# Joins before the feed-forward stages: post-norm, norm and scaling as separate steps in another order

## The chip, the cores and the metric

The kernel runs on one core of a Trainium2 chip. The metric is the device time of one execution in microseconds (us). A core has five engines that this text names: PE (TensorE, the matrix engine), DVE (VectorE), ACT (ScalarE), POOL (GpSimd) and SP (SyncE, which here only issues DMAs). Each works through its own list of instructions in order, and semaphores tie the lists together.

## The reference

Two transformer blocks run one after the other on 256 tokens of width 1024, all in float32. Only the ends of the mixers and the feed-forward parts matter here:

```
def rms_norm(x, g):
    xf = x.astype(jnp.float32)
    y = xf * lax.rsqrt(jnp.mean(xf * xf, axis=-1, keepdims=True) + NORM_EPS)
    return (y * g.astype(jnp.float32)).astype(x.dtype)

# first block (272 tokens until the mixers, 256 after)
mixed = (gate_a * y_a + gate_b * y_b) @ w_out[l]
h = h + rms_norm(mixed, mix_post_g[l])
u = rms_norm(h, ffn_pre_g[l])
gt, up = jnp.split(u @ w_ffn_in[l], 2, axis=-1)
h = h + rms_norm((jax.nn.silu(gt) * up) @ w_ffn_out[l], ffn_post_g[l])

# second block
x = x + _rms_norm(mix @ w_out[l], attn_post_norm[l])
h = _rms_norm(x, ffn_pre_norm[l])
x = x + _rms_norm(_conv_ffn(h, ffn_w_gate[l], ffn_w_up[l], ffn_conv_w[l], ffn_conv_b[l], ffn_w_down[l]), ffn_post_norm[l])
```

`_conv_ffn` is `(gelu(conv3(h @ w_gate) + b) * (h @ w_up)) @ w_down` with 4096 hidden columns.

## The kernel before

**Weights.** Every float32 product is made from parts: a weight `w` is split into `hi` (a copy rounded to fp32r) and `lo = w - hi`, and likewise each activation. Weights come from memory in slabs of 128x2048 into three buffers `raw0` to `raw2`; each half of a slab is a **unit** (128x1024, eight 128x128 blocks). For each unit u one engine makes `hi` (tile `wh`, "copy") and another makes `lo` (tile `wl`, "subtraction"). The string `MADE` says who: `d` is lo on DVE and hi on ACT, `p` lo on POOL and hi on ACT, `v` both on DVE, `q` lo on POOL and hi on DVE. The step `("split", u)` is where both are issued. SP asks for slab s+3 when both units of slab s are split.

**Order.** One list, `ORDER`, of named steps is walked by every engine's function (`tensor`, `scalar`, `vector`, `gpsimd`, `sync`); each emits its own part of a step. So the place of a step in the list fixes its place on every engine. The list is woven by `weave` from a main line (matmul steps) and side chains, by the strings in `MIX`, where a dot takes the next main step and a letter the next step of a chain.

**The joins.** Each of the four output products (`out1`, `ffn1`, `out2`, `ffn2`) ends in a join. Tokens come in two halves c = 0, 1 of 128 and columns in two halves h = 0, 1 of 512. For each c the chain made by `chains` is:

- `post(c,0)`, `post(c,1)`: ACT squares the accumulator (tile `pb`) and sums the row; DVE makes a partial mean (128x1) and multiplies the accumulator by the output factors (`FA<-pb,post`); after h = 1 ACT takes the square root and DVE the reciprocal.
- `res(c)`: DVE adds the scaled product to the residual, `X<-FA,st,X`, two instructions.
- `norm(c)`: ACT squares both halves of X, DVE makes the partial mean, ACT the root, DVE the reciprocal; then ACT scales the first half (`FA<-X,st`) and DVE the second.
- `turn(x,c)`: PE transposes the scaled rows (8 matmuls, line L509); `op(x,c,0)`, `op(x,c,1)`: ACT makes eight 128x128 `hi` parts (`R<-pb,sm`), DVE eight `lo` parts (`R<-pb,sm,R`).

PE meanwhile ends the output product with four `tail(name,c,h)` steps of 12 matmuls, then does `turn(x,0)`, then `gemm0` of the first four feed-forward tiles with token half 0 only (32 matmuls of 256 columns), then `turn(x,1)`, then `gemm1` of the same four tiles (64 matmuls). After that come full tiles of 16 matmuls, `gemm(g2,i)` and `gemm(u2,i)`, and from i = 4 on a `down` of 12.

**The tiles' banks.** Gate and up tiles of the second feed-forward go round four PSUM banks. Tile i+2 takes the bank that tile i had, and waits until step `hidden(i)` has emptied it: ACT copies one half of the bank, DVE adds the other (`FA<-pb,FA`), first for the gate tile and, three instructions later, for the up tile. `hidden(0)` comes in the list after the splits that stand behind the join.

## Time and profile before

| | |
|---|---|
| median of 3 runs | 923.08 us (923.01 to 923.38) |
| the profiled execution | 922.91 us |
| its span, first to last instruction | 921.1 us |
| PE busy | 901.0 us, 98% of the span |
| DVE, ACT, POOL busy | 671.3 us (73%), 466.2 us (51%), 214.1 us (23%) |
| mean granted clock of PE | 0.997 of full speed |
| join `out1` into the first feed-forward | about 316 to 334 us |
| join `out2` into the second feed-forward | about 631 to 650 us |

The page of the profile lists each engine's busy time; a timeline lists instructions in order of time, equal neighbours merged; windows give busy time and granted clock of a stretch. "Idle before" in brackets is how long the engine stood still ahead of a row and who let it go.

### The profile page before, as it was taken

The page shows a single profiled execution, that of the slowest core. Times are in us where ns is not written, and L with a number is a line of the kernel's source. Part 1 is how long each engine was busy: PE and PEld are TensorE (multiplying, and loading weights), DVE is VectorE, ACT ScalarE, POOL GpSimd, SP SyncE. Part 2 cuts the span into 40 slices and gives each one's busy share as a digit, 9 for nine tenths or more (in the row PEclk, how much of TensorE's full clock was granted, in tenths as well). Part 3 has the DMA queues.
Part 4 walks back from the last instruction along what each step waited for, and adds up shares of the span by engine and source line. Part 5 has one row for each costly group of instructions (what it writes and reads, how often), then busy time and mean ns, then how long its engine had stood idle before and what let it go on. Part 6 is the DMA issues. An engine that isn't in the chain of part 4 may idle for free.

```text
span 921.1 us, 16817 instructions
## 1 busy us (share of the span) xinstructions
PE 901.0 (98%) x6767; PEld 799.8 (87%) x6767; DVE 671.3 (73%) x1277; ACT 466.2 (51%) x937; POOL 214.1 (23%) x116
## 2 busy tenths in 40 slices
PE   8999999999999999999999999999999999999996
PEld 8879999989999888888888799877988888888885
DVE  6625987557656888766676668858888888788885
ACT  7443336555443574444435647776634445544343
POOL 4123421531222210652214342231101211210121
PEclk9999999999999999999999999999999999999999
DMA  8535443333333645656545354224445555455531
GB/s 318 197 138 184 139 164 114 115 116 136 117 138 132 231 163 190 221 183 223 190 162 203 137 204 164 96 79 180 166 168 195 183 197 210 153 217 183 214 106 46
DMA packets 23181, 153.67 MB, mean 167 GB/s; under 512 B 2864, under 2 KB 3248, under 8 KB 5568
## 3 DMA queue, kind: packets, MB, share of 16 engines
q1 hardware_dynamic: 22384, 150.43, 45.9%
q0 software_dynamic: 576, 2.10, 0.6%
q8 instruction: 54, 0.88, 0.4%
q14 instruction: 23, 0.19, 0.1%
q10 hardware_dynamic: 144, 0.07, 0.0%
HBM read 151.28 MB, written 1.05 MB: 165 GB/s over the span
## 4 chain that ended last, share of the span: by engine, by line
PE 62%; DVE 24%; ACT 9%; issue 4%; DMA 0%; DVEq 0%; SPq 0%; ACTq 0%
PE pb L506 60%; DVE wl L515 10%; ACT wh L512 4%; DVE FA L515 4%; DVE FA L521 4%; ACT FA L512 3%; DVE FA L518 3%; PE pb L509 2%; DVE wh L530 1%; ACT R L512 1%; DVE X L521 1%; DVE R L521 1%; DVE st L518 0%; DMA X<-in_x 0%; DVE FA L524 0%
## 5 line engine op out<-in xcount | busy, mean ns | idle before, releaser
L506 PE MATMUL pb<-R,wh 128*128 128x256 f32 (+2 forms) x2224 | 550.4, 326 | 4.5 <-ACT R L512 2.0
L506 PE MATMUL pb<-R,wl 128*128 128x256 f32 (+1 forms) x1512 | 422.6, 281 | 0.0
L506 PEld LDWEIGHTS pb<-R,wh 128*128 128x128 f32 x2224 | 372.3, 189 | 43.8 <-ACT R L512 3.5
L515 POOL TENSOR_TENSOR wl<-raw,wh 128x1024 fp32r<-128x1024 f32 (+1 forms) x76 | 185.1, 2439 | 635.7 <-ACT wh L512 513.0
L515 DVE TENSOR_TENSOR wl<-raw,wh 128x1024 fp32r<-128x1024 f32 (+1 forms) x202 | 266.9, 1343 | 84.5 <-ACT wh L512 82.8
L506 PEld LDWEIGHTS pb<-R,wl 128*128 128x128 f32 x1512 | 284.3, 188 | 2.1 <-issue 0.4
L512 ACT ACTIVATE wh<-raw 128x1024 fp32r<-128x1024 f32 (+1 forms) x220 | 223.8, 1044 | 52.4 <-PE pb L506 50.1
L506 PE MATMUL pb<-wh,R 128*128 128x512 f32 (+2 forms) x724 | 234.4, 388 | 3.4 <-DVE R L515 2.1
L506 PEld LDWEIGHTS pb<-wh,R 128*128 128x128 f32 (+1 forms) x724 | 134.4, 186 | 35.9 <-ACT R L512 4.0
L512 ACT ACTIVATE FA<-pb 128x256 f32<-128x256 f32 (+7 forms) x240 | 94.0, 414 | 124.3 <-PE pb L506 113.2
L506 PE MATMUL pb<-wl,R 128*128 128x512 f32 (+2 forms) x372 | 143.4, 385 | 0.0
L512 ACT ACTIVATE FA<-FA 128x256 f32<-128x256 f32 (+4 forms) x69 | 28.0, 405 | 139.7 <-DVE FA L521 121.8
L515 DVE TENSOR_TENSOR FA<-pb,FA 128x256 f32<-128x256 f32 (+1 forms) x128 | 53.9, 427 | 34.7 <-ACT FA L512 34.7
L506 PEld LDWEIGHTS pb<-wl,R 128*128 128x128 f32 (+1 forms) x372 | 68.2, 183 | 12.5
L515 DVE TENSOR_TENSOR FA<-FA 128x256 f32<-128x256 f32 (+7 forms) x120 | 68.7, 597 | 8.2 <-ACT FA L512 2.6
L506 PE MATMUL pb<-FA 128*32 128x16 f32 (+6 forms) x1456 | 60.9, 216 | 0.2
L512 ACT ACTIVATE R<-FA 128x256 fp32r<-128x256 f32 (+1 forms) x66 | 28.4, 431 | 61.7 <-DVE FA L515 61.7
L506 PEld LDWEIGHTS pb<-FA 128*32 128x32 f32 (+3 forms) x1456 | 53.0, 132 | 7.0 <-issue 1.7
L530 DVE CAST wh<-raw 128x1024 fp32r<-128x1024 f32 (+1 forms) x58 | 44.4, 768 | 13.1 <-PE pb L506 13.1
L515 DVE TENSOR_TENSOR R<-FA,R 128x256 fp32r<-128x256 f32 (+1 forms) x58 | 26.9, 464 | 28.9 <-ACT R L512 28.9
L512 ACT ACTIVATE FA<-FA,st 128x256 f32<-128x256 f32 (+2 forms) x65 | 29.3, 453 | 9.8 <-DVE st L518 9.6
L521 DVE SCALAR_TENSOR_TENSOR FA<-FA,sm 128x255 f32<-128x255 f32 x64 | 31.0, 484 | 2.3
(122 smaller groups left out, 462.0 us busy)
## 6 DMA issues: line engine op xcount, KB each, us to landing
raw<-in_w SPq DMA_DIRECT2D x137, 1024.0 KB, 4.8
X<-in_x SPq DMA_DIRECT2D x2, 512.0 KB, 4.3
raw<-in_w SPq DMA_DIRECT2D x2, 512.0 KB, 6.6
post<-in_ffn_post SPq DMA_DIRECT2D x2, 512.0 KB, 4.5
post<-in_w POOLq DMA_DIRECT2D x2, 512.0 KB, 5.1
FA<-in_w POOLq DMA_DIRECT2D x2, 512.0 KB, 8.2
out<-X SPq DMA_DIRECT2D x4, 256.0 KB, 2.0
cst<-in_cst SPq DMA_DIRECT2D x1, 821.5 KB, 12.3
```

The costliest lines, as they stand in the source:

```text
L506: return self.real.matmul(*a, **k) if self.real else self
L509: return self.real.transpose(*a, **k) if self.real else self
L512: return self.real.activation(*a, **k) if self.real else self
L515: return self.real.tensor_tensor(*a, **k) if self.real else self
L518: return self.real.tensor_scalar(*a, **k) if self.real else self
L521: return self.real.scalar_tensor_tensor(*a, **k) if self.real else self
L530: return self.real.tensor_copy(*a, **k) if self.real else self
```

## The change

The step `post` is cut in two. What stays in `post` is ACT's square with its sum (and the root after h = 1) and DVE's partial mean; the multiplication by the output factors and the reciprocal become `gain`. The step `norm` is cut in two: the squares, partial mean and root stay, and the reciprocal and both scalings become `scaled`. The new strings of `MIX` place these steps; in `ffn1` and `ffn2` the parts follow one another as before, in `out1` and `out2` they don't. A table `LATE` moves the subtraction of two units (87 and 183) behind another step. In `MADE`, unit 183 goes from `v` to `d`: its copy is now ACT's.

```
-    return [[("post", name, c, 0), ("post", name, c, 1), ("res", name, c)]
-            + ([("norm", name, c), ("turn", x, c), ("op", x, c, 0), ("op", x, c, 1)] if x else []) for c in range(2)]
+    return [[("post", name, c, 0), ("gain", name, c, 0), ("post", name, c, 1), ("gain", name, c, 1), ("res", name, c)]
+            + ([("norm", name, c), ("scaled", name, c), ("turn", x, c), ("op", x, c, 0), ("op", x, c, 1)] if x else [])
+            for c in range(2)]
...
-    "out1": "............c.cac..aacbab.a.aa..bb.bcbbcc.c...",
+    "out1": "............c.caac..aaacabab.abb.aa.b.bb.bcbbcc.c...",
...
-    "out2": "c.cac.a.a.aca.bcaa..bbc.bbcbbc....",
-    "ffn2": "aaa..b.bb.",
+    "out2": "c.caac.aa.ac.aababbb.aa.b.bb.bcbbcc.c...",
+    "ffn2": "aaaaa..bb.bbb.",
...
+LATE = {87: ('norm', 'out1', 0), 183: ('scaled', 'out2', 0)}
+for _u, _s in LATE.items():
+    ORDER.insert(ORDER.index(_s) + 1, ("low", _u))
...
+                elif kind == "scaled":
+                    name, c = a
+                    x = {"out1": "x2", "ffn1": "x3", "out2": "x4"}[name]
                     e.wait_ge(*dve.at(("rstd", x, c)))
                     e.activation(fa(2048 + 1024 * c, 512), X[:, 1024 * c:1024 * c + 512], ACT.Identity,
                                  scale=stat(("rstd", x, c))).then_inc(*act.up(("xn", x, c, 0)))
...
+            def low(a):
+                u = a[0]
+                c, _, hi = unit_cols(a)
+                e.wait_ge(*(act if hi == "act" else dve).at(("hi", *a)))
+                e.tensor_tensor(WL[PLACE[u]][:, c], rawu(u)[:, c], rf(WH[PLACE[u]][:, c]),
+                                ALU.subtract).then_inc(*dve.up(("lo", *a)))
...
-                    if lo == "dve":
-                        e.wait_ge(*(act if hi == "act" else dve).at(("hi", *a)))
-                        e.tensor_tensor(WL[PLACE[u]][:, c], rawu(u)[:, c], rf(WH[PLACE[u]][:, c]),
-                                        ALU.subtract).then_inc(*dve.up(("lo", *a)))
+                    if lo == "dve" and u not in LATE:
+                        low(a)
+                elif kind == "low":
+                    low(a)
...
                 elif kind == "post":
                     name, c, h = a
+                    if h == 0:
+                        e.wait_ge(*act.at(step))
+                        e.tensor_scalar(stat(("post_part", name, c)), stat(("post_ss", name, c), 2)[:, 0:1], 1.0 / D, EPS,
+                                        ALU.mult, ALU.add).then_inc(*dve.up(("post_part", name, c)))
+                elif kind == "gain":
+                    name, c, h = a
                     e.wait_ge(*in_post[name].at("all"))
                     e.wait_ge(*pe.at(("tail", name, c, h)))
-                    e.wait_ge(*act.at(step))
-                    if h == 0:
-                        e.tensor_scalar(stat(("post_part", name, c)), stat(("post_ss", name, c), 2)[:, 0:1], 1.0 / D, EPS,
-                                        ALU.mult, ALU.add).then_inc(*dve.up(("post_part", name, c)))
+                    e.wait_ge(*act.at(("post", name, c, h)))
                     e.tensor_tensor(fa(1024 * c + 512 * h, 512), acc(name, c, h)[:, :], post[:, 512 * h:512 * h + 512],
                                     ALU.mult).then_inc(*dve.up(("gained", name, c, h)))
                     banks.ended(("acc", name, c, h), dve.now())
```

PE's and POOL's own lists stay as they are, instruction for instruction. The splits of units 184 to 188 stand elsewhere. In the list before: 184 ahead of `op(x4,0)`, 185 ahead of `norm(out2,1)`, 186 between `turn(x4,1)` and `op(x4,1)`, then 187 and 188 behind. In the list after: 184 between `turn(x4,1)` and `op(x4,1)`, then 185, 186, 188, 187 behind. Units 184 and 186 have their subtraction on POOL, 185, 187 and 188 on DVE; 186 has its copy on DVE, the others on ACT.

**DVE in `out1`**, from the residual of token half 0 to the scaling of that half (pb6 and pb7 are the accumulators of half 1, wl7 is unit 87). Before:

```order
L521 SCALAR_TENSOR_TENSOR X<-FA,st,X 128x512 x2
L515 TENSOR_TENSOR wl7<-raw1,wh7 128x1024
L518 TENSOR_SCALAR st<-st 128x1
L515 TENSOR_TENSOR FA<-pb6,post 128x512
L518 TENSOR_SCALAR st<-st 128x1
L533 RECIPROCAL st<-st 128x1
L518 TENSOR_SCALAR FA<-X,st 128x512
L515 TENSOR_TENSOR FA<-pb7,post 128x512
```

And after, at the same place:

```order
L525 SCALAR_TENSOR_TENSOR X<-FA,st,X 128x512 x2
L522 TENSOR_SCALAR st<-st 128x1
L519 TENSOR_TENSOR wl7<-raw1,wh7 128x1024
L522 TENSOR_SCALAR st<-st 128x1
L537 RECIPROCAL st<-st 128x1
L522 TENSOR_SCALAR FA<-X,st 128x512
L519 TENSOR_TENSOR FA<-pb6,post 128x512
L519 TENSOR_TENSOR FA<-pb7,post 128x512
```

The norm's partial mean now stands ahead of the subtraction, and the factors of pb6 behind the scaling.

**DVE in `out2`**, from the operands of token half 0 to the first instruction of `hidden(0)` (`FA<-pb,FA`). Before:

```order
L521 SCALAR_TENSOR_TENSOR R<-pb,sm,R 128x128 x8
L515 TENSOR_TENSOR FA<-pb,post 128x512
L533 RECIPROCAL st<-st 128x1
L521 SCALAR_TENSOR_TENSOR X<-FA,st,X 128x512 x2
L515 TENSOR_TENSOR wl<-raw,wh 128x1024
L518 TENSOR_SCALAR st<-st 128x1
L533 RECIPROCAL st<-st 128x1
L518 TENSOR_SCALAR FA<-X,st 128x512
L530 CAST wh<-raw 128x1024
L521 SCALAR_TENSOR_TENSOR R<-pb,sm,R 128x128 x8
L515 TENSOR_TENSOR wl<-raw,wh 128x1024 x2
L515 TENSOR_TENSOR FA<-pb,FA 128x256
```

And after:

```order
L525 SCALAR_TENSOR_TENSOR R<-pb,sm,R 128x128 x8
L525 SCALAR_TENSOR_TENSOR X<-FA,st,X 128x512 x2
L522 TENSOR_SCALAR st<-st 128x1
L537 RECIPROCAL st<-st 128x1
L522 TENSOR_SCALAR FA<-X,st 128x512
L525 SCALAR_TENSOR_TENSOR R<-pb,sm,R 128x128 x8
L519 TENSOR_TENSOR wl<-raw,wh 128x1024
L534 CAST wh<-raw 128x1024
L519 TENSOR_TENSOR wl<-raw,wh 128x1024 x2
L519 TENSOR_TENSOR FA<-pb,FA 128x256
```

The last factors and their reciprocal went ahead of the first operands; one subtraction (unit 185) and one copy (unit 186) went from ahead of the second operands to behind them.

## Rows read from the trace of the kernel before

**Rows 1.** The page's part 1, PE: busy us, share of span, instructions.

```profile
PE 901.0 (98%) x6767; PEld 799.8 (87%) x6767; DVE 671.3 (73%) x1277; ACT 466.2 (51%) x937; POOL 214.1 (23%) x116
```

**Rows 2.** Windows: stretch, us, busy by engine, granted clock, DMA share, GB/s.

```profile
643.70:646.60 2.90, 2.90 (x14) 2.90 (x15) 2.87 (x5) 2.46 (x6) 0.00 (x0) 0.50 0.44 184
...
908.00:910.00 2.00, 2.00 (x10) 1.68 (x9) 0.75 (x2) 0.21 (x2) 0.00 (x0) 1.00 0.00 0
```

**Rows 3.** Timeline of PE: start us, us, engine, line, operation; idle before in brackets.

```profile
327.35 4.99 PE L506 MATMUL pb<-R,wh 128*128 128x256 f32 x32 [0.69 <-DVE R L521]
...
639.41 1.04 PE L509 MATMUL pb<-cst,FA 128*128 128x128 f32 x8
641.90 6.37 PE L506 MATMUL pb<-R,wh 128*128 128x256 f32 x32 [1.45 <-ACT R L512]
648.42 1.09 PE L509 MATMUL pb<-cst,FA 128*128 128x128 f32 x8
```

**Rows 4.** Timeline of PE: starts of gate tile 2 and up tile 4; a late idle.

```profile
657.56 0.40 PE L506 MATMUL pb<-R,wh 128*128 128x512 f32 x1
...
671.70 0.40 PE L506 MATMUL pb<-R,wh 128*128 128x512 f32 x1
...
906.56 0.47 PE L506 MATMUL pb<-wh,R 128*128 128x512 f32 x1 [2.10 <-DVE R L515]
```

**Rows 5.** Timeline of ACT in join `out1`.

```profile
322.55 0.62 ACT L512 ACTIVATE FA<-X 128x512 f32<-128x512 f32 x1
...
324.79 0.72 ACT L512 ACTIVATE FA<-X,st 128x512 f32<-128x512 f32 x1 [0.23 <-DVE st L533]
```

**Rows 6.** Timeline of DVE in join `out1`.

```profile
320.89 1.42 DVE L521 SCALAR_TENSOR_TENSOR X<-FA,st,X 128x512 f32<-128x512 f32 x2
...
326.86 2.14 DVE L521 SCALAR_TENSOR_TENSOR R<-pb,sm,R 128x128 fp32r<-128x128 f32 x8
```

**Rows 7.** Timeline of ACT in join `out2`.

```profile
638.48 0.72 ACT L512 ACTIVATE FA<-X,st 128x512 f32<-128x512 f32 x1 [0.23 <-DVE st L533]
...
639.68 1.05 ACT L512 ACTIVATE wh<-raw 128x1024 fp32r<-128x1024 f32 x1
...
647.64 0.72 ACT L512 ACTIVATE FA<-X,st 128x512 f32<-128x512 f32 x1 [0.23 <-DVE st L533]
648.89 2.17 ACT L512 ACTIVATE R<-pb,sm 128x128 fp32r<-128x128 f32 x8 [0.53 <-PE pb L509]
```

**Rows 8.** Timeline of DVE in join `out2`.

```profile
635.75 1.41 DVE L521 SCALAR_TENSOR_TENSOR X<-FA,st,X 128x512 f32<-128x512 f32 x2
...
641.41 2.15 DVE L521 SCALAR_TENSOR_TENSOR R<-pb,sm,R 128x128 fp32r<-128x128 f32 x8
643.61 0.69 DVE L515 TENSOR_TENSOR FA<-pb,post 128x512 f32<-128x512 f32 x1
...
644.40 1.42 DVE L521 SCALAR_TENSOR_TENSOR X<-FA,st,X 128x512 f32<-128x512 f32 x2
645.73 1.22 DVE L515 TENSOR_TENSOR wl<-raw,wh 128x1024 fp32r<-128x1024 f32 x1
```

**Rows 9.** Timeline of DVE behind join `out2`: `hidden(0)` and, last row, `hidden(2)`.

```profile
652.04 2.44 DVE L515 TENSOR_TENSOR wl<-raw,wh 128x1024 fp32r<-128x1024 f32 x2 [0.59 <-ACT wh L512]
654.40 0.42 DVE L515 TENSOR_TENSOR FA<-pb,FA 128x256 f32<-128x256 f32 x1
...
669.77 0.42 DVE L515 TENSOR_TENSOR FA<-pb,FA 128x256 f32<-128x256 f32 x1
```

**Rows 10.** Timelines of DVE and POOL: a copy and two subtractions meet POOL.

```profile
883.37 0.69 DVE L530 CAST wh<-raw 128x1024 fp32r<-128x1024 f32 x1
884.09 4.56 DVE L515 TENSOR_TENSOR wl<-raw,wh 128x1024 fp32r<-128x1024 f32 x2
...
884.03 2.40 POOL L515 TENSOR_TENSOR wl<-raw,wh 128x1024 fp32r<-128x1024 f32 x1 [23.32 <-ACT wh L512]
...
648.81 2.38 POOL L515 TENSOR_TENSOR wl<-raw,wh 128x1024 fp32r<-128x1024 f32 x1 [5.65 <-DVE wh L530]
```

More of the change, by code:

```diff
@@ L412 @@
 MADE = ("dpdpddddddddqdpdpdddpddpvpvdppqpdddppddddpddvqpqpqpdpdvddpdddpqddvdpddppddpddpddpddvvdddqvddddpd"
-        "ddvvvdvdppdpdppvvpdqpdpqvddpvpdvpdddvpdvpdvdddvqdddqqpddpdpvddvdddddddpvvvdppvpppdvvdddvpdqddddd"
+        "ddvvvdvdppdpdppvvpdqpdpqvddpvpdvpdddvpdvpdvdddvqdddqqpddpdpvddvdddddddpvvvdppvpppdvvddddpdqddddd"
         "pvddvddddvdddvdpqpdddddddqddddddddddddddppddpddddddqddddvddvdvddddddpdvvdddvdvpdddpp")
@@ L418 @@
     "latent": "...a.......a..a...........a.b....b.fgf.b..e.f.g.e.dc.f.ba...c.ge.i.cg.ecdh.dh....i...i.h.d.ih",
-    "out1": "............c.cac..aacbab.a.aa..bb.bcbbcc.c...",
-    "ffn1": "..aaa..aa..c....caac....bbc..b..b..b.b...b............",
+    "out1": "............c.caac..aaacabab.abb.aa.b.bb.bcbbcc.c...",
+    "ffn1": "..aaaaa..aaa..c....caac....bbbbc..b..bb..b.b...b............",
     "maps": "...a.....acbabcbc..cc.bbb.ede.eed.ecag.agcdgcggadc.b.bfcgbefdc.ab.dgfbe.dbhffbab.hcfhcccf.ghiecb"
             "eif.gahf.ddib.b.bbigchjbj.i.cbcibhhcjkhajkhckkhcjbiiibjcbijkicjgikc.kjjjkk.kkijg.k.",
-    "out2": "c.cac.a.a.aca.bcaa..bbc.bbcbbc....",
-    "ffn2": "aaa..b.bb.",
+    "out2": "c.caac.aa.ac.aababbb.aa.b.bb.bcbbcc.c...",
+    "ffn2": "aaaaa..bb.bbb.",
 }
@@ L1888, in vector @@
                     x = {"out1": "x2", "ffn1": "x3", "out2": "x4"}[name]
-                    r = stat(("rstd", x, c))
                     e.wait_ge(*act.at(("norm", name, c, 0)))
@@ L1892, in vector @@
                                     ALU.mult, ALU.add).then_inc(*dve.up(("norm_part", x, c)))
+                elif kind == "scaled":
+                    name, c = a
+                    x = {"out1": "x2", "ffn1": "x3", "out2": "x4"}[name]
+                    r = stat(("rstd", x, c))
                     e.wait_ge(*act.at(("sd", x, c)))
```

## The prediction

> **What bounds the kernel now.** I read first the page's busy times: PE is busy 98% of the span [rows 1], so only what makes PE stand still, or stretches its work, can move the time. Next I listed who PE waited for, stretch by stretch. Inside the two feed-forward stages that list is empty but for the last tiles; PE stands in the joins. In `out1` it stands ahead of the first transposes and again 0.69 us before `gemm0`; the 32 matmuls of `gemm0` then take 4.99 us. In `out2` it stands 1.45 us, and the same 32 matmuls take 6.37 us [rows 3]. Windows laid over that stretch say why: from 643.70 to 646.60 the granted clock is 0.50, so PE ran at 1.2 GHz and not at 2.4 [rows 2]; it is the only such place while PE works. What PE had done before was to transpose (1.04 us) [rows 3], to stand 1.45 us, and to go at the pace of the operands for two more. The price is 6.37 - 4.99 = 1.4 us, but it was nearly hidden: the transposes of token half 1 start at 648.42 [rows 3], and the scaled rows were not there until 647.64 + 0.72 = 648.36 anyhow [rows 7].
>
> So each join has two halves: until `gemm0` starts, and until `turn(x,1)` starts. After that comes a third thing, how far DVE is behind PE at the start of the feed-forward, and there the change puts new work.
>
> **Part 1, join `out1`.** Before, ACT squared X from 322.55 and scaled it at 324.79 [rows 5]; DVE had begun X at 320.89 [rows 6], then came a subtraction (1.22 us, as in rows 8), the factors of pb6 and the partial mean. With nothing in between, the path from X to scaling takes 638.48 - 635.75 = 2.73 us [rows 7, 8], so scaling could come at 323.62: the gain is at most 1.17 us, and at least nothing. What stays in between now: the root on ACT is done about 2.2 us after X begins (323.1), then the square of pb6 (0.6 us and its sum) is ahead of the scaling in ACT's list, and DVE's partial mean of it, which waits for that square, is ahead of the reciprocal. That gives 323.3 + 0.7 for the square, 0.15 for the mean, 0.2 for the reciprocal: scaling at 324.4, 0.4 us earlier. DVE's postponed subtraction ends at 323.7, inside this. Behind the scaling both lists hold what they held (square and root of pb7 on ACT, factors of pb7 on DVE; the factors of pb6, 0.7 us, are in time before pb7's square is). So the first operands, at 326.86 before [rows 6], come 0.4 us earlier, and everything behind them shifts alike, since no clock loss stands in this join. **-0.4 us** (bounds 0 and -1.17; near the middle of neither, because I counted the list off). The feed-forward stage behind it is PE's alone, so the gain is carried on.
>
> **Part 2, join `out2` until `gemm0`.** DVE loses a copy of 0.69 (unit 183 goes to ACT, where it fills a wait of 1.4 us ahead of the squares of X) and gains the factors of pb3 (0.69 us) [rows 8] ahead of the first operands. ACT loses the copy of unit 184 (1.05 us) [rows 7] and gets the square and root of pb3 (0.9 us). The two sums cancel: operands again at 641.4, PE again stands 1.45 us. **0.**
>
> **Part 3, join `out2` until the second transposes.** Behind the first operands (8 instructions from 641.41, 2.15 us) DVE now goes straight to X: 643.5 in place of 644.40; and the subtraction of 1.22 us between X and the partial mean is gone [rows 8]. With the clear path of 2.73 us scaling starts at 643.5 + 2.7 = 646.2 in place of 647.64 [rows 7]: 1.4 us earlier, and the rows are there at 646.95. When PE takes them depends on its clock:
> - at 1.2 GHz again, `gemm0` ends at 648.27 (the transposes' start less 0.15 us that PE stood) and the gain is 0.15 us;
> - at 2.4 GHz, `gemm0` ends at 641.90 + 4.99 = 646.9 (the row of the other join), the transposes start at 646.97, but ACT is then in the copy of unit 184, 1.05 us from 646.8 on, which stood elsewhere before. ACT could start on operands 648.89 - 648.42 = 0.47 us after the transposes begin [rows 3, 7] and starts at 647.8, 0.35 us later. Gain 1.45 - 0.35 = 1.1 us.
>
> PE's list and its first idle are the same as before, so I take the low clock as the likelier. **-0.15 us** (the other end -1.1).
>
> **Part 4, DVE behind the join.** Before, DVE did two subtractions, 652.04 to 654.48, and then `hidden(0)` [rows 9]. Now it does a subtraction (unit 185), a copy (186), and two subtractions (188, 187). By their plain rows that is 1.2 + 0.7 = 1.9 us more. But the copy also releases POOL's subtraction of unit 186. Before, this ran at 648.81 for 2.38 us, beside the second operands, which are read from PSUM and were not held up. Now it meets DVE's subtractions. The row for exactly this row of instructions stands at the end of the stage: copy at 883.37, two subtractions from 884.09 that take 4.56 us where a free pair takes 2.44, with POOL busy from 884.03 for 2.40 [rows 9, 10]. So from the first subtraction's start at 652.04: 1.22 us, then 884.09 + 4.56 - 883.37 = 5.28 us, end at 658.5 and not 654.5. **DVE is 4.0 us later** (bounds: 1.9 with no meeting, 4.2 if both subtractions are held).
>
> [...]
>
> Nothing in `hidden(0)` to `hidden(2)` lets DVE catch up: its pauses there are waits for ACT's step inside the same chain. What PE can stand is the least distance between the emptying of a bank and the tile that wants it. Tiles start every 16 matmuls: gate 2 at 657.56, up 4 at 671.70 [rows 4]. DVE's additions for their banks end at 654.82 and 670.19 [rows 9]: distances of 2.7 and 1.5 us; of the four banks between, none has less than 1.5. With 0.1 us for the signal, DVE has 1.4 us to give. PE stands 4.0 - 1.4 = **+2.6 us** in all, in three pieces: about 1.4 at gate 2, 0.8 at gate 3 and 0.4 at up 4. From tile 5 on the distance grows, so it doesn't go further. The copies that are needed for these tiles are all earlier; slab loads come later by 6 us for one slab, which still lands some 4 us ahead of its copy, as that copy too is behind `hidden(0)`.
>
> **Sum.** -0.4 + 0 - 0.15 + 2.6 = +2.0 us. On the profiled execution's span, 921.1 + 2.0 = 923.1, and with the 1.8 us around it 924.9; the median shown is 0.17 us above the profiled run, so 925.1. I say **925.0**.
>
> **Rivals.**
> - *The clock stays up in `out2`* (part 3, second case), all else alike: -0.4 - 1.1 + 2.6 = +1.1, 924.1. For it: in `out1` a very similar stretch kept 2.4 GHz. Against: the stretch that lost it is unchanged.
> - *Not slower: DVE's delay stays under what it has to give.* The one place is `hidden(0)`; the price is 4.0 us if POOL's subtraction of unit 186 meets DVE's, 1.9 if DVE gets both of its own through first. At 1.9 PE stands 0.5 us: -0.4 - 0.15 + 0.5 = -0.05, or -1.0 with the clock up: 922.1 to 923.0. It decides at a delay of 1.4 + 0.55 = 1.95 us. For it: the same copy releases both, and DVE needs no signal from another engine. Against: the rows of 883 us.
> - *PE's new pauses bring the clock down once more*: +1.4 us, the price of the row at 641.90, 926.4. Against: a pause of 2.10 us at 906.56 in dense work kept the clock, 1.00 behind it [rows 2, 4].
> - *The reordering does nothing in `out1`* because the square of pb6 is as late as before: 0.4 us more, 925.4.
> - *A clear gain*, over 1.85 us: needs both joins at their best (-1.17 and -1.1) and no stall; the traces give nothing for all three.
>
> **How the numbers follow.** Forecast with low clock 0.40; clock up 0.27; delay absorbed 0.17; second clock loss 0.10; the rest 0.06. The range takes the first two with their bounds of some 0.6 us, the second clock loss, and half of the third: 922.4 to 926.4. A change of 0.2% (1.85 us) is about what a measurement of this kernel can tell from none. The forecast lies just beyond that bound: of its 0.40 some 0.25 is beyond and 0.15 within; the clock-up and absorbed cases are within, the second clock loss is beyond. Slower 0.38, same 0.57, faster 0.05.
>
> **What would show it.** In the trace of after: transposes of `out1` near 325.15, and `gemm0` at 326.95; in `out2`, with all 0.4 earlier, ACT's second scaling 1.4 us earlier than 647.2, and `gemm0` either about 5.0 or 6.4 us long. Behind the join, POOL busy beside DVE's subtractions, one of them 3.3 to 3.4 us long; then idle of PE, released by DVE's `FA`, at three tile starts between 655 and 673, 2.6 us together, where there was none. If that idle is missing, part 4 is wrong, and the kernel is no slower. If the `hidden` steps come late but the idle is under 1 us, what DVE has to give was misread.

## The result, and the profile after

| | before | after |
|---|---|---|
| median | 924.50 us (922.81 to 925.92, 19 executions) | 927.47 us (924.98 to 929.25, 19 executions) |
| ratio, 95% interval | | 1.0028 [1.0020, 1.0037] |
| the profiled execution, its span | 922.91, 921.1 us | 925.02, 923.2 us |

The change makes the kernel 0.28% slower, about 2.6 us. The executions of one kernel fall into a lower and an upper group of times, of before near 922.7 to 923.9 and 924.3 to 926.1 us, of after 924.98 to 925.43 (5 of 19) and 926.6 to 929.3 (14 of 19). The 923.08 us shown ahead of the prediction came from three executions of the lower group. Both profiled executions, 922.91 and 925.02, are of the lower groups and 2.1 us apart; how the upper groups come about is a second matter, told below.

In the changed kernel the lines of the old file stand four lower: L506 is L510 (matmul), L509 L513 (transposes), L512 L516, L515 L519, L518 L522, L521 L525, L530 L534. In experiments 3 and 10 they stand four lower again.

**The page of after**: busy times of PE and the others, and the chain of waits by engine.

```profile
PE 900.7 (98%) x6767; PEld 798.6 (87%) x6767; DVE 672.3 (73%) x1276; ACT 467.3 (51%) x938; POOL 215.3 (23%) x116
...
PE 77%; DVE 13%; ACT 7%; issue 2%; DMA 0%; DVEq 0%; SPq 0%; ACTq 0%
```

PE works as long as before (901.0 in [rows 1]), in a span 2.1 us longer: it stands still for that time. **The timeline of PE after**, at the places of [rows 3, 4] and wherever it stood still behind them (start us, us, engine, line, operation, idle before in brackets):

```profile
326.60 1.64 PE L510 MATMUL pb<-R,wh 128*128 128x256 f32 x6 [0.69 <-DVE R L525]
...
641.25 4.99 PE L510 MATMUL pb<-R,wh 128*128 128x256 f32 x32 [1.38 <-ACT R L516]
646.33 1.09 PE L513 MATMUL pb<-cst,FA 128*128 128x128 f32 x8
648.01 0.36 PE L510 MATMUL pb<-R,wh 128*128 128x256 f32 x1 [0.59 <-ACT R L516]
...
657.00 0.47 PE L510 MATMUL pb<-R,wh 128*128 128x512 f32 x1 [1.06 <-issue]
...
663.53 0.47 PE L510 MATMUL pb<-R,wh 128*128 128x512 f32 x1 [0.65 <-issue]
...
672.42 0.47 PE L510 MATMUL pb<-R,wh 128*128 128x512 f32 x1 [0.17 <-ACT FA L516]
...
908.64 0.47 PE L510 MATMUL pb<-wh,R 128*128 128x512 f32 x1 [3.36 <-DVE R L519]
```

Read it as a ledger against [rows 3, 4]. `gemm0` of `out1` starts at 326.60, 0.75 us earlier than 327.35; 0.24 us of that is there from the first microseconds of the program on and is not the change's. `gemm0` of `out2` starts 0.65 earlier, its transposes 2.09 earlier (646.33 against 648.42). Then come the three waits at tile starts, and the last wait has grown from 2.10 to 3.36 us. **Windows of PE after**, over `gemm0` of `out2` and behind the last wait (stretch, us, PE busy, granted clock, DMA share, GB/s):

```profile
643.70:646.60 2.90, 2.81 (x24) 1.00 0.49 179
908.60:912.00 3.40, 3.36 (x15) 1.00 0.02 5
```

Where [rows 2] had 0.50 there is 1.00: in this execution PE kept 2.4 GHz in `out2`, and it kept it behind the last wait too.

**DVE and ACT after in `out1`**, from X to the scaling of token half 0, the places of [rows 5, 6]:

```profile
320.68 1.42 DVE L525 SCALAR_TENSOR_TENSOR X<-FA,st,X 128x512 f32<-128x512 f32 x2
...
323.09 0.58 ACT L516 ACTIVATE FA<-pb 128x512 f32<-128x512 f32 x1
...
324.05 0.72 ACT L516 ACTIVATE FA<-X,st 128x512 f32<-128x512 f32 x1 [0.29 <-DVE st L537]
```

**DVE, ACT and POOL after in and behind `out2`**, the places of [rows 7 to 9]:

```profile
645.55 0.72 ACT L516 ACTIVATE FA<-X,st 128x512 f32<-128x512 f32 x1 [0.23 <-DVE st L537]
646.18 1.04 ACT L516 ACTIVATE wh<-raw 128x1024 fp32r<-128x1024 f32 x1
647.13 2.15 ACT L516 ACTIVATE R<-pb,sm 128x128 fp32r<-128x128 f32 x8
...
650.26 1.22 DVE L519 TENSOR_TENSOR wl<-raw,wh 128x1024 fp32r<-128x1024 f32 x1 [0.59 <-ACT wh L516]
...
652.01 4.56 DVE L519 TENSOR_TENSOR wl<-raw,wh 128x1024 fp32r<-128x1024 f32 x2
656.49 0.41 DVE L519 TENSOR_TENSOR FA<-pb,FA 128x256 f32<-128x256 f32 x1
...
652.17 3.31 POOL L519 TENSOR_TENSOR wl<-raw,wh 128x1024 fp32r<-128x1024 f32 x1 [2.48 <-DVE wh L534]
```

The pair of subtractions takes 4.56 us beside POOL, where [rows 9] had 2.44 without it, and `hidden(0)` starts at 656.49 where it started at 654.40: 2.09 us later. That number comes back at every later `hidden` step. Here are two instructions **of before**, the scaling in `hidden(20)` and the last operand, of `hidden(31)`, that PE waits for:

```profile
813.56 2.04 DVE L518 TENSOR_SCALAR FA<-FA,sm 128x256 f32<-128x256 f32 x1
...
905.99 0.43 DVE L515 TENSOR_TENSOR R<-FA,R 128x256 fp32r<-128x256 f32 x1 [0.48 <-ACT R L512]
```

and the same two **of after**:

```profile
815.62 2.04 DVE L522 TENSOR_SCALAR FA<-FA,sm 128x256 f32<-128x256 f32 x1
...
908.07 0.43 DVE L519 TENSOR_TENSOR R<-FA,R 128x256 fp32r<-128x256 f32 x1 [0.48 <-ACT R L516]
```

They are 2.06 and 2.08 us later. (The scaling of 2.04 us is another meeting with POOL; in `hidden(0)` it takes 0.41.) Over 250 us and 32 tiles DVE's list gains nothing back, while PE is only 0.81 us late from 680 us on. So at the end PE waits 1.3 us longer, and the whole 2.1 us are in the span. **The chain of waits of before between 651 and 907 us, by line**, says why:

```profile
by line: DVE wl L515 34.2%; ACT wh L512 12.4%; DVE FA L521 12.4%; DVE FA L515 9.8%; DVE FA L518 9.8%; issue 9.0%; ACT FA L512 5.5%; DVE wh L530 4.5%; ACT R L512 2.0%; DVE R L515 0.4%; PE pb L506 0.2%
```

PE has 0.2% of it. From the first subtraction behind `out2` to the last `hidden` step the path that sets the end ran through DVE (and ACT's copies that DVE waits for), not through PE, although PE was busy nearly all the time. I had read only who PE waits for.

### The profile page after: what moved, and what is told of

It reads as the page before. It is cut to its first block, busy times and chain, and to the rows that moved or that the text cites. A ratio compares the mean times of both kernels' runs of the same rounds, so it can differ in the third digit from the quotient of the medians.

```text
span 923.2 us, 16813 instructions
## 1 busy us (share of the span) xinstructions
PE 900.7 (98%) x6767; PEld 798.6 (87%) x6767; DVE 672.3 (73%) x1276; ACT 467.3 (51%) x938; POOL 215.3 (23%) x116
## 4 chain that ended last, share of the span: by engine, by line
PE 77%; DVE 13%; ACT 7%; issue 2%; DMA 0%; DVEq 0%; SPq 0%; ACTq 0%
PE pb L510 75%; DVE wl L519 5%; ACT FA L516 3%; DVE FA L519 2%; ACT wh L516 2%; PE pb L513 2%; DVE FA L525 2%; DVE FA L522 1%; ACT R L516 1%; DVE wh L534 1%; DVE X L525 1%; DVE R L525 1%; ACT L516 0%; DMA X<-in_x 0%; DVE st L522 0%
## 5 line engine op out<-in xcount | busy, mean ns | idle before, releaser
L510 PE MATMUL pb<-R,wh 128*128 128x256 f32 (+2 forms) x2224 | 549.4, 326 | 6.6 <-ACT R L516 2.2
L510 PE MATMUL pb<-R,wl 128*128 128x256 f32 (+1 forms) x1512 | 422.7, 281 | 0.0
L510 PEld LDWEIGHTS pb<-R,wh 128*128 128x128 f32 x2224 | 370.8, 188 | 46.7 <-ACT R L516 3.8
L519 POOL TENSOR_TENSOR wl<-raw,wh 128x1024 fp32r<-128x1024 f32 (+1 forms) x76 | 186.2, 2453 | 636.8 <-ACT wh L516 517.5
L519 DVE TENSOR_TENSOR wl<-raw,wh 128x1024 fp32r<-128x1024 f32 (+1 forms) x202 | 269.0, 1354 | 84.4 <-ACT wh L516 82.7
L510 PEld LDWEIGHTS pb<-R,wl 128*128 128x128 f32 x1512 | 284.2, 188 | 2.1 <-issue 0.4
L516 ACT ACTIVATE wh<-raw 128x1024 fp32r<-128x1024 f32 (+1 forms) x221 | 224.8, 1044 | 52.6 <-PE pb L510 50.5
L510 PE MATMUL pb<-wh,R 128*128 128x512 f32 (+2 forms) x724 | 234.4, 388 | 4.7 <-DVE R L519 3.4
L510 PEld LDWEIGHTS pb<-wh,R 128*128 128x128 f32 (+1 forms) x724 | 134.4, 186 | 37.2 <-ACT R L516 5.2
L516 ACT ACTIVATE FA<-pb 128x256 f32<-128x256 f32 (+7 forms) x240 | 94.2, 414 | 123.9 <-PE pb L510 112.8
L510 PE MATMUL pb<-wl,R 128*128 128x512 f32 (+2 forms) x372 | 143.4, 385 | 0.0
L516 ACT ACTIVATE FA<-FA 128x256 f32<-128x256 f32 (+4 forms) x69 | 28.0, 405 | 142.4 <-DVE FA L525 125.3
L519 DVE TENSOR_TENSOR FA<-pb,FA 128x256 f32<-128x256 f32 (+1 forms) x128 | 53.9, 426 | 35.4 <-ACT FA L516 35.4
L510 PEld LDWEIGHTS pb<-wl,R 128*128 128x128 f32 (+1 forms) x372 | 68.3, 184 | 12.5
L519 DVE TENSOR_TENSOR FA<-FA 128x256 f32<-128x256 f32 (+7 forms) x120 | 68.2, 593 | 8.2 <-ACT FA L516 1.9
L510 PE MATMUL pb<-FA 128*32 128x16 f32 (+6 forms) x1456 | 60.9, 216 | 0.2
L516 ACT ACTIVATE R<-FA 128x256 fp32r<-128x256 f32 (+1 forms) x66 | 28.4, 431 | 61.3 <-DVE FA L519 61.3
L510 PEld LDWEIGHTS pb<-FA 128*32 128x32 f32 (+3 forms) x1456 | 53.0, 132 | 7.0 <-issue 1.5
L534 DVE CAST wh<-raw 128x1024 fp32r<-128x1024 f32 (+1 forms) x57 | 43.8, 769 | 13.1 <-PE pb L510 13.1
L519 DVE TENSOR_TENSOR R<-FA,R 128x256 fp32r<-128x256 f32 (+1 forms) x58 | 27.0, 465 | 28.9 <-ACT R L516 28.9
L516 ACT ACTIVATE FA<-FA,st 128x256 f32<-128x256 f32 (+2 forms) x65 | 29.3, 454 | 9.8 <-DVE st L522 9.6
L525 DVE SCALAR_TENSOR_TENSOR FA<-FA,sm 128x255 f32<-128x255 f32 x64 | 30.9, 484 | 2.3
```

What stands on the lines that cost most here:

```text
L510: return self.real.matmul(*a, **k) if self.real else self
L516: return self.real.activation(*a, **k) if self.real else self
L519: return self.real.tensor_tensor(*a, **k) if self.real else self
L525: return self.real.scalar_tensor_tensor(*a, **k) if self.real else self
L534: return self.real.tensor_copy(*a, **k) if self.real else self
```

## The experiments

All are timed against the kernel before on the same chip. "The changed kernel" is that of after.

**1. The changed kernel again**, unaltered.

> The changed kernel, unaltered, for a second profile and more single times. In its first profile the span was 923.2 us with the clock at 2.4 GHz through both joins, but most of its executions were near 926 us of span at a mean clock of 0.995 to 0.997. Theory A (PE loses its clock in the pauses that the change added behind join out2, or in the join itself): the slow executions have the lower mean clock; a profile of one has a stretch at 0.50 between 640 and 675 us and PE's starts behind it are later by about half of that stretch. Theory B (the slower executions come from DMA or from a slower DVE): the time does not go with the clock. Ratio to the kernel before 1.002 to 1.004.

Measured: 926.98 us (926.76 to 928.04, 7 executions), ratio 1.0027 [1.0017, 1.0038]; the span profiled was 926.2. PE's timeline and windows of this execution at its last wait:

```profile
908.79 0.76 PE L510 MATMUL pb<-wh,R 128*128 128x512 f32 x1 [3.40 <-DVE R L519]
```

```profile
908.80:911.00 2.20, 2.20 (x5) 0.50 0.03 7
911.00:914.50 3.50, 3.50 (x10) 0.50 0.00 0
```

Up to the wait everything is as in after (`hidden(0)` at 656.63, the same three waits, DVE late by the same amount); behind it PE goes at 1.2 GHz for about 6 us, and the last matmul starts 3.0 us later than in the profile of after. That is an execution of the upper group, and its mean clock is lower, as theory A has it (0.996 against 0.998); but the place is not the one that theory A named, between 640 and 675 us. **Its chain of waits from 651 to 908 us**:

```profile
by line: DVE wl L519 35.3%; DVE FA L525 12.3%; ACT wh L516 12.0%; DVE FA L519 9.8%; DVE FA L522 9.8%; issue 8.9%; ACT FA L516 5.4%; DVE wh L534 4.7%; ACT R L516 1.9%; DVE R L519 0.2%
```

It has no PE at all. The chain in the profile of after goes over PE between 672 and 820 us; with DVE's steps late by the same 2.1 us on both sides of 820, I take that for two releasers close together and go by the steps. No run settles it by itself; experiment 8 bears it out.

**2. Only `out1` new**: `out2` as before.

```diff
-    "out2": "c.caac.aa.ac.aababbb.aa.b.bb.bcbbcc.c...",
+    "out2": "c.caac.aa.a.aaca.bbcaa..bbbc.bbbcbbc....",
...
-LATE = {87: ('norm', 'out1', 0), 183: ('scaled', 'out2', 0)}
+LATE = {87: ('norm', 'out1', 0)}
```

(with the letter of unit 183 back to `v`).

> Only join out1 in the new order; join out2 and all splits as before. In the first profile of the changed kernel PE's starts behind join out1 had moved by 0.54 us against those ahead of it. Theory: 0.5 us less than before, 0.9994 to 0.9996 of it, if nothing behind gives it back. Rival (the end of the kernel hangs on something that doesn't start at this join): no change, 1.000.

Measured: 924.15 us (922.70 to 926.68, 11), ratio 1.000 [0.999, 1.001]. From PE's timeline, the second transposes of `out2` and the last wait:

```profile
647.82 1.09 PE L513 MATMUL pb<-cst,FA 128*128 128x128 f32 x8 [1.63 <-ACT FA L516]
...
906.32 0.47 PE L510 MATMUL pb<-wh,R 128*128 128x512 f32 x1 [2.43 <-DVE R L519]
```

No waits at tile starts. The first row is worth a look: here too PE kept 2.4 GHz in `out2`, and then waited 1.63 us for the scaled rows. So the 1.4 us of the clock loss in [rows 3] were hidden indeed; the old order pays nothing for them. PE and DVE are both 0.58 us early through the whole stage, 0.53 of it from `out1`; but DVE loses 0.33 us in `hidden(26)` (a wait for ACT's part of the step that before did not have), and the end is 0.21 us early. On PE join `out1` gives 0.5 us where the prediction said 0.4. What of it reaches the time, the ratio of 1.000 cannot tell: theory (0.9994 to 0.9996) and rival both lie in its interval.

**3. The splits of units 185 and 186 back** ahead of the second operands, all else as changed.

```diff
+ORDER.remove(('split', 185))
+ORDER.insert(ORDER.index(('norm', 'out2', 1)), ('split', 185))
+ORDER.remove(('split', 186))
+ORDER.insert(ORDER.index(('op', 'x4', 1, 0)), ('split', 186))
```

> The changed kernel, but the splits of units 185 and 186 back at their places ahead of the second operands of join out2 (a subtraction between X and the partial mean, a copy between scaling and operands). Theory D (DVE's list is one path from join out2 to the end, so what stands behind the join is paid in full there, partly by pauses at the tile starts and the rest in PE's wait ahead of the last four down tiles): the pauses of 1.06, 0.65 and 0.17 us at the tile starts are gone, PE's wait near the end is back from 3.36 to about 2.1 us, the join gives back about 1.2 us; span about 4.0 - 1.2 = 2.8 us less than the changed kernel in the same clock state, 0.997 of it, that is 0.999 to 1.000 of the kernel before. Rival E (only the tile starts hang on DVE, as predicted; the last 1.3 us come from elsewhere): 2.6 - 1.2 = 1.4 us less, and the wait near the end stays at 3.4.

Measured: 925.47 us (924.54 to 926.13, 11), ratio 1.0011 [1.0002, 1.0020], span 923.4. PE's second transposes and last wait, DVE's first subtractions behind the join with ACT's copies and POOL beside them, and the window behind the last wait:

```profile
647.22 1.09 PE L517 MATMUL pb<-cst,FA 128*128 128x128 f32 x8 [0.69 <-ACT FA L520]
...
907.24 0.47 PE L514 MATMUL pb<-wh,R 128*128 128x512 f32 x1 [3.36 <-DVE R L523]
...
652.37 2.79 DVE L523 TENSOR_TENSOR wl<-raw,wh 128x1024 fp32r<-128x1024 f32 x2 [1.81 <-ACT wh L520]
...
651.28 2.01 ACT L520 ACTIVATE wh<-raw 128x1024 fp32r<-128x1024 f32 x2 [1.11 <-PE pb L514]
...
648.20 4.74 POOL L523 TENSOR_TENSOR wl<-raw,wh 128x1024 fp32r<-128x1024 f32 x2 [27.52 <-ACT wh L520]
```

```profile
907.90:910.50 2.60, 2.60 (x8) 0.50 0.03 6
```

The three waits at tile starts are gone, PE is 0.59 us early from 680 us on, and all the same the ratio stays above 1. Two of its numbers are those of rival E: the last wait is still 3.36 us, and the median is 1.5 us below that of experiment 1 (925.47 against 926.98), not 2.8. Theory D had expected `hidden(0)` back at its old place. It is 0.68 us later than before (0.9 against the end of `ffn1`), for the edit does not restore the old list whole: unit 188 stays ahead of 187, and 184 behind the transposes. DVE's first subtraction starts 0.33 us later, behind a copy of ACT that has waited 1.11 us for PE, and the pair takes 2.79 us and not 2.44, beside POOL, which has two subtractions in a row until 652.9. The 0.68 us stay to the end, and the wait is what it was before plus both shifts, 2.10 + 0.59 + 0.68 = 3.37 us. PE cannot keep its gain; DVE's 0.7 us decide, and the clock is low behind the wait. So the steps speak for theory D, and the run's own numbers alone would not; experiments 8 and 9 decide. It was the first sign that what PE does in the stage does not count.

**4. No meeting with POOL**: the copy and subtraction of unit 186 both on DVE (`q` to `v`).

> The changed kernel, but the subtraction of unit 186 is made by DVE itself and not by POOL. DVE does 1.22 us more and meets no POOL there. Theory D with the collision priced at 2.2 us: DVE is 2.2 - 1.2 = 1.0 us earlier than in the changed kernel at hidden(0), pauses at tile starts together 0.9 and not 1.9 us, end 1.0 us earlier. Rival (POOL and DVE don't hold each other up there): 1.2 us later than the changed kernel.

Measured: 927.02 us (925.60 to 927.57, 11), ratio 1.0024 [1.0016, 1.0033], span 924.4. DVE behind the join, PE's second gate tile, and the window behind the last wait (of 3.65 us):

```profile
652.51 3.50 DVE L519 TENSOR_TENSOR wl<-raw,wh 128x1024 fp32r<-128x1024 f32 x3
...
656.44 0.47 PE L510 MATMUL pb<-R,wh 128*128 128x512 f32 x1
```

```profile
908.90:911.00 2.10, 2.10 (x6) 0.50 0.03 8
```

Three subtractions in 3.50 us where two took 4.56: one more instruction and still 1.06 us less. Against the end of `ffn1`, `hidden(0)` comes 0.9 us earlier than in after, and of the waits at tile starts one of 0.68 us is left. So the meeting cost what [rows 10] said. Of the 0.9 us 0.65 are left at `hidden(31)` (0.3 go in `hidden(26)`, as in experiment 2). In the time the gain does not show: the median of 927.02 is beside 926.98 in experiment 1 and 927.47 in the result, and the expected 1.0 us is missed. PE gained more than DVE and waits longer at the end, 3.65 us, and no execution is under 925.60, where after had five. So the gain is shown at DVE's steps and not in the time.

**5. Filler in the last wait**: 12 matmuls into an idle bank, between the third and the fourth k of the first `tail` of `ffn2`.

```diff
+                    if (name, c, h) == ("ffn2", 0, 0):
+                        for k in ks[:-1]:
+                            down(name, k, c, False, False, (h,))
+                        b = bank("filler", (4, 5, 6, 7))
+                        for i in range(12):
+                            e.matmul(b[:, :], R2[:, 0:128], R2[:, 0:512], start=True, stop=True)
```

> The changed kernel, with 12 matmuls of 512 columns into an idle bank put into PE's last wait (the one of 3.36 us ahead of the last down products of token half 0). Each takes 0.21 us at 2.4 GHz, 2.6 us together, so they lie wholly in the wait and PE then stands about 0.8 us there; they add nothing to the path, and the profiled span stays at 923.2, as that of the changed kernel. Theory (the length of this wait is what brings the clock to 1.2 GHz behind it in most executions): granted clock 1.00 up to the last matmul, and the median falls from about 927.2 to about 925.2, a ratio of 1.0007 to the kernel before. Rival (executions differ in their clock by something else than this wait): the low clock behind 908 comes as often as before, median again about 927, ratio 1.002 to 1.003.

Measured: 925.71 us (924.90 to 926.59, 11), ratio 1.0009 [1.0000, 1.0017], span 924.8. PE's `gemm0` of `out2` with the transposes behind it, the filler, what follows, and the window from there:

```profile
641.94 6.53 PE L510 MATMUL pb<-R,wh 128*128 128x256 f32 x32 [1.38 <-ACT R L516]
648.31 1.03 PE L513 MATMUL pb<-cst,FA 128*128 128x128 f32 x8
...
906.72 2.92 PE L510 MATMUL pb<-R 128*128 128x512 f32 x12
910.21 0.47 PE L510 MATMUL pb<-wh,R 128*128 128x512 f32 x1 [0.57 <-DVE R L519]
```

```profile
910.20:914.00 3.80, 3.79 (x17) 1.00 0.02 4
```

Useless work makes the kernel 1.3 us faster in the median than in experiment 1 (1.7 us by the two ratios): no execution is above 926.6 any more, where after had 14 of 19. With the wait all but filled the low clock behind it is gone, so it is the wait that brings the clock down. The expected 925.2 was missed by 0.5 us, and the first row says for what: in this execution the clock fell in `gemm0` of `out2` (as in [rows 2]). In the old order that is hidden. In the new one the scaled rows are ready before, so nothing hides it: `gemm1` starts 7.69 us behind `gemm0` and not 6.76, and `hidden(0)` 16.17 us behind it and not 15.24, as in the profile of after. **0.9 us**, in those executions in which it happens; with the filler they are, by their times, probably the ones from 925.7 to 926.6, and their mean clock, 0.997 to 0.998 against 0.999 in the other five, agrees. (The rest by which this profile is longer than that of after is drift ahead of the join: it reaches the end of `ffn1` 0.7 us later.)

**6. `out1` new, and the last down products in another order**: for token half 0, k = 28 to 30 of both column halves ahead of k = 31 of either.

```diff
+                    if name == "ffn2" and c == 0:
+                        if h == 0:
+                            for hh in range(2):
+                                for k in ks[:-1]:
+                                    down(name, k, 0, False, False, (hh,))
+                        m, u = down(name, ks[-1], 0, False, True, (h,))
```

> Only the join out1 is new (as in r2_out1_only), and in the last stage the down products of k=28 to 30 are taken for both token halves before that of k=31: 24 matmuls, about 5 us of work, that stood behind PE's wait for hidden(31), now stand ahead of it. Theory (DVE's list is what sets the end, and PE's last wait of 2.43 us is its slack): the wait is filled with work that has to be done anyway, and the end comes 2.1 to 2.4 us earlier than in r2_out1_only, at a span of about 918.6; the clock stays 1.00 to the end; median about 922, ratio 0.9975. Rival (what is behind the wait is bound by the output's own chain on DVE, ACT and the store, so that PE's order doesn't matter): the span stays within 0.5 us of 920.9 and the ratio at 1.000.

Measured: 920.58 us (920.47 to 921.11, 5), ratio 0.9954 [0.9941, 0.9966], span 919.3. PE's last wait:

```profile
906.78 0.47 PE L510 MATMUL pb<-wh,R 128*128 128x512 f32 x1 [0.52 <-DVE R L519]
```

What is moved is k = 28 to 30 of column half 1 of token half 0 (not of the other token half, as the expectation words it): 9 matmuls, 2.0 us, and not 24. They fill the wait of 2.4 us but for 0.5, and the end comes 1.6 us earlier than in experiment 2 (2.1 against the end of `ffn1`, which this execution reached 0.5 us later). The median falls by 3.6 us, because the executions with a low clock behind the wait are, by their times, gone as well: the five lie within 0.7 us. The rival, with the span within 0.5 us of 920.9, is out.

**7. The changed kernel with the same order of the last products.**

> The changed kernel with the same order of the last down products as r6_out1_tail. Theory (the last 1.3 us of the change's cost and its loss of clock both are this one wait of 3.36 us): the wait vanishes, the end comes 3.0 to 3.4 us earlier than in the changed kernel, span about 920.0, no low clock, median about 922.5, ratio 0.998; the difference to r6_out1_tail is then what stands at the three tile starts less what out2 gained, 0.8 + 0.6 = 1.4 us. Rival (DVE's delay of 2.1 us goes to the output in any case): the span stays above 922.5.

Measured: 923.41 us (922.73 to 924.25, 11), ratio 0.9988 [0.9979, 0.9996], span 922.4. `gemm0` of `out2` and the last wait on PE:

```profile
641.55 6.54 PE L510 MATMUL pb<-R,wh 128*128 128x256 f32 x32 [1.38 <-ACT R L516]
...
909.83 0.47 PE L510 MATMUL pb<-wh,R 128*128 128x512 f32 x1 [1.33 <-DVE R L519]
```

That is 3.6 and 4.1 us less than the two medians of the changed kernel. The wait does not vanish, as I had expected with the wrong count of matmuls: 3.36 less 2.0 is 1.3. It kept its clock. The two kernels with this tail differ only by the new `out2`: 2.8 us in the median, 3.1 in the profiled executions. Expected were 1.4; it is more since PE still waits for DVE at the end in both, and with the low clock in `out2`, as both profiles have it, DVE's last operand is 3.3 us later here than in experiment 6 against the end of `ffn1`.

**8. A shorter list for DVE**: `out1` new, and nine units of the last stage no longer subtracted by POOL: 192, 207, 232, 270, 274, 275 from `p` to `d`, 208, 217, 243 from `q` to `v`. In the trace of before POOL's subtraction of each ran beside a subtraction or a scaling of DVE and made that 1.4 to 2.2 us longer than its free row, as with the scaling of 2.04 us shown above.

> Only the join out1 is new (as in r2_out1_only), and in the last stage nine units of a weight whose split POOL did (wholly or in part) beside a DVE subtraction are split by DVE and ACT alone. Each such meeting makes a DVE instruction 1.4 to 2.2 us longer, but the unit's own subtraction of 1.2 us comes to DVE for six of them. Theory (DVE's list from out2 to the end is one path): its last hidden step comes 3 to 5 us earlier than in r2_out1_only, PE's last wait of 2.43 us is gone, the end comes 2.0 to 2.4 us earlier, span 918.5 to 918.9, ratio 0.9975. Rival (DVE's list has room that these meetings use up): the last hidden step moves under 1 us and the end with it.

Measured: 920.02 us (919.83 to 920.38, 5), ratio 0.9946 [0.9933, 0.9960], span 918.5. DVE's last operand, and **the chain of waits from 651 to 905 us**:

```profile
901.33 0.43 DVE L519 TENSOR_TENSOR R<-FA,R 128x256 fp32r<-128x256 f32 x1 [0.48 <-ACT R L516]
```

```profile
by line: PE pb L510 100.1%
```

Nine subtractions more for DVE, and its last operand comes 4.4 us earlier (901.33 against 905.74 in experiment 2). The chain has gone over to PE altogether, and PE stands nowhere in the stage. The span is 2.4 us shorter than in experiment 2, which is the wait of 2.43 us, as the theory had it; the median falls by 4.1, more than expected, as the low clock behind the wait is gone with it. This shows directly that DVE was the bound.

**9. The changed kernel with these nine units.**

> The changed kernel, with the nine units of the last stage made as in r8_out1_made, so that DVE's list becomes some 4 us shorter behind the first tiles. Theory (the cost of the change is 1.4 us at the first tile starts, where DVE's list is late by what stands ahead of hidden(0), and 1.3 us and a loss of clock at PE's last wait, where the whole list is late): the three waits at tile starts stay as they are, the last wait of 3.36 us vanishes, and the end comes 1.4 us later than in r8_out1_made where out2 keeps 2.4 GHz (span about 919.9) and 2.3 us later where it falls to 1.2 GHz (920.8); no low clock at the end; median 921.7 to 922.6, ratio 0.997 to 0.998. Rival (the change's cost at the end has a cause of its own, such as the later slab loads): over 2.5 us behind r8_out1_made in an execution at full clock, span above 921.

Measured: 922.57 us (921.87 to 923.74, 11), ratio 0.9978 [0.9969, 0.9987], span 920.6. The waits of 1.07 and 0.65 us at the first two tile starts are still there, the last wait is gone, and there is one new wait on PE:

```profile
670.59 0.47 PE L510 MATMUL pb<-R,wh 128*128 128x512 f32 x1 [0.70 <-DVE FA L519]
```

It has unit 192's subtraction behind it, which is DVE's now and comes ahead of `hidden(2)`. From 680 us on PE is 1.9 us late against the end of `ffn1`, and it ends 1.93 us behind experiment 8 against the same mark. Expected were 1.4; the new wait makes the difference. With DVE out of the way, the end pays what the tile starts cost less what `out2` gains and no more: this execution shows no other cost of the change.

**10. Both joins new, splits back, nine units.**

> Both joins new, the two splits back ahead of the second operands (as in r3_splits_back), and the nine units as in r8_out1_made. Theory: with the splits back no tile start waits, and with DVE's list shorter there is no last wait, so what the new order of out2 gives PE (0.4 us in the trace of r3_splits_back, behind the join) reaches the end: 0.4 us ahead of r8_out1_made, span about 918.1, median 919.6, ratio 0.994 to 0.995. Rival (out2's new order gives nothing that reaches the end): equal to r8_out1_made within 0.1 us or behind it.

Measured: 920.17 us (919.88 to 920.77, 5), ratio 0.9958 [0.9944, 0.9971], span 919.0. It is not ahead of experiment 8, as the rival has it, but with five executions each and overlapping intervals 0.4 us could not be told from nothing. In the execution profiled the clock was low in `out2`:

```profile
643.90:647.00 3.10, 3.10 (x16) 0.50 0.15 61
```

and PE is then as late behind the join as before (+0.05 us). At 2.4 GHz the new order was 0.4 us ahead there (experiment 3). Whether that reaches the end in such executions no profile here shows; it would be less than these times can tell.

**11. The kernel before again.**

> The kernel before, unaltered. It tells how far two sets of executions of one kernel lie apart here: ratio 1.000 with an interval of about 0.001. Theory (PE's last wait of 2.1 us brings the clock down in part of the executions already before the change): executions in two groups, near 922.8 and near 925, and if the profiled one is of the second, its clock is 0.50 for some us behind the wait at 906.6. Rival (the second group is something else): clock 1.00 behind the wait in a profile with a span above 922.3.

Measured: 924.55 us (923.01 to 925.76, 11) against 924.68 (922.73 to 926.12, 21), ratio 1.0002 [0.9994, 1.0011], span 922.7. PE's last wait and the windows behind it:

```profile
906.53 0.47 PE L506 MATMUL pb<-wh,R 128*128 128x512 f32 x1 [2.32 <-DVE R L515]
```

```profile
907.80:910.50 2.70, 2.70 (x7) 0.50 0.00 0
911.50:914.00 2.50, 2.50 (x13) 1.00 0.00 0
```

The kernel before loses its clock at this wait too, and by their times (7 of 11 are 924.38 us or more) in the larger part of its executions. The profile ahead of the prediction, with 1.00 behind a wait of 2.10 us, happened to be one that didn't.

## Why the prediction was wrong

It said 925.0, between 922.4 and 926.4; the median is 927.47. Of the 2.5 us by which it missed, 1.4 are the base, 923.08 and not 924.50; the change itself was forecast at +1.9 and measured +2.6 by the ratio, +3.0 by the medians. By its steps, each against the mark ahead of it, in the profile of after:

| step | predicted | measured |
|---|---|---|
| 1, `out1` | -0.4 | -0.5 (also in experiments 1 to 10) |
| 2, `out2` until `gemm0` | 0 | -0.1 |
| 3, until the second operands, 1.2 GHz | -0.15 | -0.2 (experiments 5, 7) |
| 3, the same at 2.4 GHz | -1.1 | -1.1 (the profile of after) |
| 4, from DVE's first subtraction to `hidden(0)` | +4.0 | +3.9 (6.23 us, before 2.36) |
| 4, PE at the tile starts | 1.4, 0.8, 0.4: +2.6 | 1.3, 0.9, 0.4: +2.6 |
| behind it | 0 | +1.3 |
| clock behind the last wait | kept | lost in most executions |

The sizes in parts 1 to 4 held within 0.2 us, part 3 in both of its cases. (Each of the three waits moved what is behind it by 0.2 us more than its own length, which is how 1.06, 0.65 and 0.17 become 2.6.) The Trainium skill, page "SBUF — State Buffer", section "SBUF: two separate sides", says of the port pair that DVE and GpSimd share that, where a DVE instruction has two inputs in SBUF and the GpSimd one reads SBUF, the one that comes second is blocked until the first has ended. This case agrees, with 4.56 us for a pair of subtractions beside POOL in after and 3.50 us for three without it.

**The step that failed** stands near the end of part 4: "From tile 5 on the distance grows, so it doesn't go further." The distance at tile starts does grow. But PE has one more thing to take from DVE, the last `hidden` product, and that distance was already used up: the wait of 2.10 us at 906.56, which I had among my rows [rows 4] and had used only as evidence on the clock, is PE waiting for DVE. A list that PE waits for at the end has nothing "to give". The 1.4 us that DVE was said to have to give were lent, and were paid at 908. The chain of waits, DVE and the copies that it waits for from 651 to 907 us, would have said so at once. The sum then is simply DVE's: its first subtraction comes 1.78 us earlier (650.26 against 652.04: 0.5 from `out1`, 1.2 from `out2`, and 0.1 that is drift outside of the joins), `hidden(0)` follows 3.87 us later behind it than before, and 3.87 - 1.78 = 2.1 us, which is what the span grew by. That the forecast's +2.0 stands close to that is luck: the 1.3 us missing at the end are offset by the 0.9 that it didn't give to `out2` at 2.4 GHz and by small sums.

**The second thing it missed** is the clock behind the last wait, with the base that hangs on it. The rival "PE's new pauses bring the clock down once more" had a chance of 0.10 and was argued away with the clock of 1.00 behind the wait of 2.10 us. It happened, at the end instead of behind the join. One execution with 1.00 behind a wait was no proof: experiment 11 shows the same kernel with 0.50 behind 2.32 us. In the seven profiles with a last wait of 2.10 us or more, the clock behind it was 1.00 in three (2.10, 2.43 and 3.36 us) and 0.50 in four (2.32, 3.36, 3.40 and 3.65 us), for some 3 to 6 us; in the six with 1.33 us or less, or none, it was 1.00. An estimate of its cost is the median less the lowest execution: 1.7 us before, 2.5 us after (in which some executions may have the 0.9 us of a low clock in `out2` as well). That, with the 2.1 us of the full-clock executions, gives +2.9. The Trainium skill, page "TensorE: Matmul & The Clock Gate", Part 1, says of a kernel's start that the number of matmuls at the low clock differs from run to run of the same kernel. These traces show the like in the middle of one, with 0 and 6 us behind the same wait of 3.4 us.

A third, small thing: the changed `out2` loses 0.9 us when its `gemm0` falls to 1.2 GHz, and the old one nothing. I had both cases, as -0.15 and -1.1, and they were right. Which of the two comes is not fixed by the order: of the 13 profiled executions 5 fell and 8 did not, the unaltered kernel before once each way. What decides it stays open.

The base of 923.08 came from three executions, all of the lower group, and a forecast made on it is one for the lower group. The five executions of after there have a median of 925.04; that this is the forecast's 925.0 is the luck told above.

## What to carry to other kernels

That PE is busy 98% and waits nowhere in a stage does not make PE its bound: if it waits for another engine where the stage ends, that engine's list may be the path through the whole stage. Here it was, and what was put on it was paid at the end, however much distance the tiles in between had. Before saying that an engine has time to give, follow the chain of waits back from the stage's end. And the first thing to do with such a last wait is to put work into it that has to be done anyway: nine matmuls taken out of the list behind it gave 3.6 us in the median, more than the whole change cost, and moving nine subtractions from POOL back to DVE gave 4.1, because each of them, run beside DVE, had cost DVE more than doing it.

## What was not expected of the hardware

- A wait of 2.3 us on PE in dense work can bring it to 1.2 GHz for some 3 us, and the same wait of 3.4 us can cost 0 or 3.0 us of the end (923.2 and 926.2 us of span, the same kernel).
- Work that is never read, 12 matmuls in the wait of 3.36 us, made the kernel 1.3 us faster in the median (experiment 5 against 1).
- Subtracting a unit costs DVE 1.22 us alone, and having POOL do it beside DVE's own cost 1.4 to 2.2 us of DVE's time, besides 2.4 us of POOL's.

The best kernels here are those of experiments 6, 8 and 10, at 0.995 to 0.996 of the time before; their intervals overlap. The two edits of 6 and 8 were not run together, since 8 leaves no wait to fill.
